# A hybrid RWKV-7, convolution and MoE layer on one core: reordered opening, moved masks, transposes and fills, and a third weight slot

## What is computed

```python
xn = rmsnorm(x, norm1_g)
z = xn @ w_in                      # 1024 x 7424: r | k | v | LoRA inputs | GLU (2 x 1024) | gates (2 x 1024)
zr_prev = previous token of z[:, :C_RWKV]           # samples: state_shift @ w_in
zm = zr + (zr_prev - zr) * mu_shift                 # r, k, v and three LoRA inputs
S = S * d_t + (S @ -kk_t) b_t^T + v_t k_t^T         # 16 heads, 64 x 64 state, per token
out_a = (groupnorm(S r_t) + bonus) * g
out_b = silu(layernorm(depthwise_conv(glu, width 31)))
h = x + (sigmoid(gA) * out_a + sigmoid(gB) * out_b) @ w_out
y = h + moe(rmsnorm(h, norm2_g))                    # top 8 of 64 experts and one shared expert
return rmsnorm(y), new states
```

## Time and profile before

| | us |
|---|---|
| median of 3 runs | 1151.5 |
| lowest, highest | 1150.77, 1154.52 |
| profiled execution | 1153.62 |
| its span, first to last instruction | 1151.8 |
| PE busy | 970.0 (84%) |
| DVE busy | 554.1 (48%) |
| POOL busy | 350.9 (30%) |
| ACT busy | 217.0 (19%) |
| mean granted TensorE clock | 0.929 of 2.4 GHz |

### The profile page before, as it was taken

The page is one execution under the profiler, slowest core; times in us unless marked ns, Lnnn a source line. Parts: engine busy times, 40 slices in busy tenths (PEclk is TensorE's granted clock), DMA queues, the critical chain, the costliest instruction groups (busy, mean ns, idle before and its releaser), DMA issues. The chain is left out here.

```text
span 1151.8 us, 17728 instructions
## 1 busy us (share of the span) xinstructions
PE 970.0 (84%) x7221; PEld 568.8 (49%) x7221; DVE 554.1 (48%) x1025; ACT 217.0 (19%) x460; POOL 350.9 (30%) x396
## 2 busy tenths in 40 slices
PE   4898899799889988579899888898888687969896
PEld 3677678767677776336633333333333233323231
DVE  2148758775884789675461111111111424333585
ACT  3231124112411421213011111111111111111002
POOL 0039705950892289000111101101112322222330
PEclk9998999899999999888999988988998888989899
DMA  8332354154306507383579999999999999999931
GB/s 249 122 110 84 126 163 129 48 185 151 111 19 220 159 3 264 126 342 152 207 278 401 417 417 413 415 414 400 408 403 399 412 409 368 406 406 402 389 101 39
DMA packets 98811, 295.65 MB, mean 257 GB/s; under 512 B 19570, under 2 KB 50740, under 8 KB 82071
## 3 DMA queue, kind: packets, MB, share of 16 engines
q1 hardware_dynamic: 80535, 254.02, 57.8%
q0 software_dynamic: 18192, 40.46, 9.7%
HBM read 284.12 MB, written 36.30 MB: 278 GB/s over the span
## 5 line engine op out<-in xcount | busy, mean ns | idle before, releaser
L1275 PE MATMUL bank<-big 64*64 64x64 f32 (+7 forms) x6778 | 914.6, 368 | 153.2 <-DMA big<-in_w_up 73.3
L1275 PEld LDWEIGHTS bank<-big 64*64 64x64 f32 (+3 forms) x6778 | 520.5, 154 | 497.9 <-issue 384.1
L1567 ACT ACTIVATE big<-bank 128x512 f32<-128x512 f32 (+11 forms) x292 | 124.7, 449 | 751.4 <-PE bank L1275 438.3
L1075 POOL DMA_INDIRECT big<-xg,big x32 | 32.4, 1013 | 405.2 <-PE bank L561 355.2
L2020 POOL TENSOR_SCALAR big<-big 128x256 f32<-128x256 f32 x120 | 129.0, 1075 | 0.4
L919 DVE TENSOR_TENSOR big<-big,bank 128x256 f32<-128x256 f32 x32 | 13.5, 421 | 234.6 <-ACT big L1567 234.6
L2032 POOL TENSOR_TENSOR big<-big 128x256 f32<-128x256 f32 x120 | 89.4, 745 | 0.3
L1845 DVE SCALAR_TENSOR_TENSOR big<-big 128x256 f32<-128x256 f32 x120 | 71.3, 594 | 4.0
L979 DVE SCALAR_TENSOR_TENSOR big<-big 128x1024 f32<-128x1024 f32 (+1 forms) x48 | 61.5, 1280 | 17.5 <-DMA big<-yrows,big 14.6
L1092 POOL DMA_INDIRECT big<-yrows,big x48 | 50.0, 1042 | 51.8 <-DVE big L979 29.5
L2016 POOL TENSOR_SCALAR big<-big 128x256 f32<-128x256 f32 x4 | 2.2, 551 | 190.5 <-DVE big L1805 190.5
(11 more groups left out here) (165 smaller groups left out, 439.5 us busy)
## 6 DMA issues: line engine op xcount, KB each, us to landing
big<-in_w_gate SPq DMA_DIRECT2D x64, 1024.0 KB, 16.1
big<-in_w_up SPq DMA_DIRECT2D x64, 1024.0 KB, 21.9
big<-in_w_down SPq DMA_DIRECT2D x64, 1024.0 KB, 15.3
big<-in_w_in SPq DMA_DIRECT2D x29, 1024.0 KB, 5.5
yrows<-big POOLq DMA_DIRECT2D x32, 512.0 KB, 6.2
big<-in_w_out SPq DMA_DIRECT2D x2, 2048.0 KB, 11.8
big<-in_x_prompt SPq DMA_DIRECT2D x2, 1024.0 KB, 7.0
big<-in_state_wkv SPq DMA_DIRECT2D x32, 64.0 KB, 2.3
```

The costliest lines, as they stand in the source:

```text
L1075: pool.indirect_dma_start(out=x[0:n, :], out_offset=None, in_=xg, in_offset=bass.IndirectOffsetOnAxis(ap=idxu[0:n, col:col + 1], axis=0), ...
L1275: return nc.tensor.matmul(out_, lhsT=lhsT, rhs=rhs, start=start, stop=stop)
L1567: return nc.scalar.activation(out_, in_, f, **kw)
```

## The change

It touches six things.

1. *Opening.* `rms_eps` moves up beside `ident`, and the first load takes only these 129 columns; the other 1421 are loaded with the LoRA weights, behind the second `w_in` piece, under the semaphore `late_in`. x is loaded in halves with the gains between. ACT makes one Sqrt before it waits for x. The waits for LoRA weights and `lora_ready` on PE move from before tile 2 to the first LoRA products. The copy of the convolution state leaves the opening (`shift_out` 48 becomes 32).
2. *Masks.* X2 moves from before the levels to behind the first Y.
3. *Transposes.* New `between`; `i % 8 % 3` starts each group with the same bank. ACT's copies follow the new order.
4. *State.* The memset of `S_st` moves ahead of T. PE's waits before the chunk loop are split up.
5. *Fills.* One after each odd tap 7 to 21; the state copy after tap 24 of group 3.
6. *Ring.* `NW` = 3.

```diff
-        NW = 2
+        NW = 3
@@ moe_pool: the fills and the state copy share one semaphore
-            pool.wait_ge(S['yrows_in'], 16 * NPAIR)
+            pool.wait_ge(S['yrows_in'], 16 * (NPAIR + 1))
@@ SP
-            sp.dma_start(const, A['const']).then_inc(S['consts_in'], 16)
-            sp.dma_start(xrow[:, 0:2, :], A['x_prompt'][0].rearrange("(t p) d -> p t d", p=128)) \
-              .then_inc(S['x_in'], 16)
+            sp.dma_start(const[:, 0:first], A['const'][:, 0:first]).then_inc(S['x_in'], 16)
+            sp.dma_start(xrow[:, 0, :], x_rows[:, 0, :]).then_inc(S['x_in'], 16)
+            sp.dma_start(grow, A['norm1_g'][0:1, :].partition_broadcast(128)).then_inc(S['small_in'], 16)
...
+            sp.dma_start(xrow[:, 1, :], x_rows[:, 1, :]).then_inc(S['hx_in'], 16)
...
-                sp.wait_ge(S['tr_free'], 8 * g + 2)
+                sp.wait_ge(S['tr_free'], 8 * g + 1)
...
                 if q == 1:
+                    sp.dma_start(const[:, first:], A['const'][:, first:]).then_inc(S['late_in'], 16)
@@ PE
             z_tile(0)
             z_tile(1)
-            pe.wait_ge(S['lora_in'], 48)
-            pe.wait_ge(S['lora_ready'], 3)
...
                 if g == 0:
                     pe.wait_ge(S['vec_ready'], 2)
+                    pe.wait_ge(S['late_in'], 64)
+                    pe.wait_ge(S['lora_ready'], 3)
...
-                pe.wait_ge(S['lmask_ready'], 4 * (g + 1))
+                pe.wait_ge(S['lmask_ready'], 4 * g + 2)
...
                 between = [
-                    lambda: (tr_units(BP), tr_samples(), tr_conv_state()),
+                    lambda: tr_samples(),
+                    lambda: (pe.wait_ge(S['lmask_ready'], 4 * (g + 1)), tr_units(BP)),
                     lambda: tr_units(KP),
                     lambda: tr_v(),
-                    lambda: tr_new_conv(),
-                    lambda: None,
+                    lambda: (tr_conv_state(), tr_new_conv()),
                 ]
...
-                pe.wait_ge(S['tt_ready'], 6 * g + 6)
-                pe.wait_ge(S['tr_free'], 8 * g + 6)
+                pe.wait_ge(S['tr_free'], 8 * g + 4)
                 pe.wait_ge(S['zero_ready'], g + 2)
...
                     pe.wait_ge(S['zq_ready'], n + 1)
+                    if c == 0:
+                        pe.wait_ge(S['tt_ready'], 6 * g + 6)
...
-                    if c:
-                        pe.wait_ge(S['o_ready'], n)
+                    pe.wait_ge(S['o_ready'], n) if c else pe.wait_ge(S['tr_free'], 8 * g + 6)
@@ ACT
-            act.wait_ge(S['consts_in'], 16)
-            act.wait_ge(S['x_in'], 16)
+            act.wait_ge(S['zero_ready'], 1)
+            fn(stat[:, 15:16], PP[:, 0, 0, 0:1], ACT.Sqrt)
+            act.wait_ge(S['x_in'], 32)
@@ DVE
-            dve.wait_ge(S['shift_out'], 48)
+            dve.wait_ge(S['shift_out'], 32)
...
+            dve.wait_ge(S['late_in'], 64)
             for g in range(NG):
...
+                note(v.memset(S_st[0], 0.0), 'zero_ready')
...
-                for h in range(2):
-                    dve.wait_ge(S['a_mm'], 5 * g + h + 4)
-                    note(v.tensor_tensor(X2[:, 4 * h:4 * h + 4],
...
                     link(v.tensor_tensor(Y_st, bank(0), bc(f'level{m}'), M), 'y_ready')
+                    if i == 0:
+                        for h in range(2):
+                            dve.wait_ge(S['a_mm'], 5 * g + h + 4)
+                            note(v.tensor_tensor(X2[:, 4 * h:4 * h + 4],
@@ POOL
-            pool.dma_start(out['conv_s'][0][:, 0:CW - 2, :], A['state_conv'][0][:, 1:CW - 1, :]) \
-                .then_inc(S['shift_out'], 16)
+            def fill(g, w):
+                i = (w - 7) // 2
+                if w % 2 and 0 <= i < NPAIR // NG:
+                    r = 2 * SLOTS * (NPAIR // NG * g + i)
+                    pool.dma_start(yrows[r:r + 2 * SLOTS, :], const[:, 0:D]).then_inc(S['yrows_in'], 16)
+                if g == NG - 1 and w == 24:
+                    pool.dma_start(out['conv_s'][0][:, 0:CW - 2, :], A['state_conv'][0][:, 1:CW - 1, :]) \
+                        .then_inc(S['yrows_in'], 16)
...
-                taps(g, 6, CW)
-                for i in range(NPAIR // NG):
-                    r = 2 * SLOTS * (NPAIR // NG * g + i)
-                    pool.dma_start(yrows[r:r + 2 * SLOTS, :], const[:, 0:D]).then_inc(S['yrows_in'], 16)
+                taps(g, 6, CW, lambda w: fill(g, w))
```

More of the change, by code:

```diff
@@ L76, in constants @@
     parts['ident'] = np.eye(128)
+    parts['rms_eps'] = np.full((128, 1), RMS_EPS)
     parts['same_head'] = (p[:, None] // 64 == p[None, :] // 64)
@@ L99, in constants @@
     parts['ln_eps'] = np.full((128, 1), LN_EPS)
-    parts['rms_eps'] = np.full((128, 1), RMS_EPS)
     off, cols = {}, 0
@@ L1282, in heads @@
                 return ins
-            pe.wait_ge(S['consts_in'], 16)
             for t in range(2):
@@ L1693, in _ @@
                 gate_tile(13)
+                copy_samples()
                 copy_units(BT_st)
-                copy_samples()
-                copy_conv_state()
                 copy_units(KTok_st)
                 copy_units(V_st)
+                copy_conv_state()
                 copy_new_conv()
@@ L1743, in _ @@
             v.memset(zs[:, :, 0:1], 0.0)
-            v.memset(C, 0.0)
             v.memset(UU[:, :, 0:CW - 1], 0.0)
             note(v.memset(PP[:, :, :, 0:1], 1.0), 'zero_ready')
+            v.memset(C, 0.0)
             dve.wait_ge(S['small_in'], 48)
@@ L1864, in _ @@
                 bank = lambda i: B[i][:, :].rearrange("p (u n) -> p u n", u=NU)
+                wait(dve, 's_mm', NCH * g)
+                wait(dve, 'o_mm', NCH * g)
+                wait(dve, 'tr_free', 8 * g)
+                note(v.memset(S_st[0], 0.0), 'zero_ready')
                 dve.wait_ge(S['a_mm'], 5 * g + 3)
@@ L1907, in sample_part @@
                         link(v.tensor_reduce(OS, SMT, AX.X, AD), 'os_ready')
-                wait(dve, 's_mm', NCH * g)
-                wait(dve, 'o_mm', NCH * g)
-                wait(dve, 'tr_free', 8 * g)
-                note(v.memset(S_st[0], 0.0), 'zero_ready')
-                dve.wait_ge(S['zero_ready'], g + 2)
                 for c in range(NCH):
@@ L2003, in _, with taps @@
             pool.dma_start(out['shift_s'][0], xrow[0:NS, 2, :]).then_inc(S['shift_out'], 16)
-            pool.dma_start(out['conv_s'][0][:, 0:CW - 2, :], A['state_conv'][0][:, 1:CW - 1, :]) \
-                .then_inc(S['shift_out'], 16)
-            def taps(g, w0, w1):
+            def fill(g, w):
[6 more added lines that the diff above has]
+                        .then_inc(S['yrows_in'], 16)
+            def taps(g, w0, w1, behind=None):
                 acc = C[:, 2 * g + 1, 0:NP]
@@ L2032, in taps @@
                     note(gp.tensor_tensor(acc, acc, TP[:, w % 3, :], ALU.add), 'tapm')
+                    if behind:
+                        behind(w)
+            pool.wait_ge(S['late_in'], 64)
             for g in range(NG):
```

29 lines of the change are left out of this document (15 added, 14 removed).

## The result

| | before | with the change |
|---|---|---|
| median of 4 executions, us | 1151.55 | 1139.38 |
| lowest, highest | 1150.77, 1154.52 | 1137.20, 1146.67 |
| profiled execution, its span | 1153.62, 1151.8 | 1146.67, 1144.9 |
| first products of groups 0, 1, 2, 3 | 76.03, 183.58, 291.13, 397.96 | 68.65, 172.84, 277.36, 382.97 |
| first expert weight issued | 493.11 | 477.24 |

The ratio is 0.988, 95% interval 0.986 to 0.991. Of the 27.4 forecast before the first expert weight, 15.9 came.

A forecast was written before the change was run, and what follows sets the result against it. PE's waits in the 493 us before the expert stage were taken as what to shorten; the DMA-busy expert stage would move forward as a block. 7.2 + 16.5 + 3.65 = 27.4 us gave 1124.1 us, range 1115 to 1136.

The forecast's parts named there:

- Part 1, the opening: Opening: earlier first weights 1.0, PE's 4.53 us gap gone, 1.7 from the clock; 7.2 us gained, bounded by 4 and 9.
- the third slot: Ring of w_in loads: the third slot itself earns nothing, since PE has no wait of note for w_in in the groups.
- Part 2, groups 0 to 2: Triangular inversion levels: moved masks, transposes and memset let PE start sooner; 4.4 us gained in each of these groups.
- The first gap: PE's wait before the first level: 2.0 us would be left.
- the t products: Levels, by group 1's clock: PE starts these products 4.8 us earlier.
- Part 2, group 3: Last group's levels: 3.3 us gained, without the 1.14 us before the chunk loop, as no projection tiles fill it.
- Part 3, the failing step: Fills between POOL's taps cost nothing, covered by idle time; PE's wait for od goes: 3.65 us, bounded by 0 and 5.
- DVE becomes the bound of the levels: Rival: DVE's work, slowed beside POOL, limits the levels; 2 us gained per group, 1132.6 us. Chance 0.17.
- Clock stays down: Rival: two scattered gaps hold PE's lower clock through the levels; 37 us slower, 1188 us. Chance 0.03.
- lost before the expert stage: Rival: another condition of the sync engine ends as late as now, so the gain vanishes; 1150 us. Chance 0.03.
- the clock stays up: Rival: PE keeps its upper clock in the levels, each group gaining 5.8 us; 1118.5 us. Chance 0.10.
- weight load behind the first was late in the opening: Rival: a weight load queues behind constants, LoRA weights and states; 5 us back, 1129 us. Chance 0.07.

The follow-up runs named there:

- opening_only: Kernel before with only the new opening, plus the convolution state copy moved behind tap 24 of group 3; 1145.3 us, ratio 0.994.
- fills_end: Changed kernel with only the fills of yrows put back to the end of each group; 1130.4 us, ratio 0.982.
- short_pool_taps: Changed kernel with POOL's taps cut to the first 8 tokens, fills still between them; 1114.7 us in one execution.
- wout_late: fills_end with w_out and the expert stage's x loaded only behind group 3's last y products; 1135.9 us, ratio 0.985.
- wout_after_od: fills_end with w_out, x and the router's loads issued behind the read-back of od of group 3; 1130.5 us, ratio 0.981.
- state_first: fills_end with DVE's sample step behind the state update and the copy of o, in group 3 only; 1131.5 us, ratio 0.981.
- wout_late_od_first: wout_late with group 3's fills issued only after od has been read back; 1126.4 us, ratio 0.977.
- again: The changed kernel run once more, unaltered; 1139.2 us, ratio 0.989.

## Why the prediction was wrong

- **Part 1, the opening: right.** 7.2 forecast; 7.4 in the profile, 7.1 by the medians of opening_only (the first products of group 0 lie between 67.6 and 69.2 us in all kernels with the new opening). The first tile came 1.6 us sooner (1.0 forecast). The gap between tiles 1 and 2 is gone, the granted clock is 1.00 from 20.2 to 60 us, the first tile came at 20.20, and the third slot earned nothing, as said.
- **Part 2, groups 0 to 2: right without the fills.** 4.4 a group forecast, 5.2, 5.1 and 4.3 in fills_end against opening_only. The first gap was 2.2 to 2.3 (forecast 2.0), the t products stood 4.5 earlier from the group's start (forecast 4.8), and no wait was left before the chunk loop. Whether the clock fell didn't matter for the first t: in group 3 the first y took 1.97 us or 1.34 (two kernels, same gap before), and the next gap was 0.73 or 1.35, so t began 3.24 and 3.25 us behind y. DVE's mask ends that wait, and a slow PE is hidden in it. By the rule of the Trainium skill ("TensorE: Matmul & The Clock Gate", section "HAM oscillation — how this bites in real kernels") the clock would have stayed up and each group gained 5.8. The trace doesn't agree: behind gaps of 2.15 to 2.29 us the clock fell in each group of fills_end, as in the kernel before, and the two best groups come near 5.8 through the order alone. What a clock that stays up gives is seen in short_pool_taps.
- **Part 2, group 3: wrong sign.** 3.3 forecast, 1.9 lost. I priced the moved steps on PE and DVE and left out what SP issues: its wait went from `8 * g + 2` to `8 * g + 1` and levels and transposes moved, so w_out was issued 31.3 us behind the group's start in fills_end instead of 36.1 before. PE then stood 1.97 + 0.77 us in the levels, and behind the first of these gaps the granted clock was 0.51 for 3 us. wout_late and wout_after_od removed exactly these gaps. That they are late fetches of PE's own instructions is an inference from the profile's "issue", not shown. The wait of 2.43 us for DVE before chunk 1 is a second cost; state_first moved it and gained nothing, so what it is worth stays open. The clock is a third: over the group it was 0.86 instead of 0.90, and the same products took PE 69.7 us instead of 66.9 in opening_only. With w_out and fills moved (wout_late_od_first) the group takes 90.1, 2.6 less than in opening_only; but 1.28 of this is the wait for `od`, so some 1.3 of the 3.3 came.
- **Part 3, the failing step.** "The taps end 4.3 us later, covered by the long idle time before POOL's first tap of the next group" costed the interleaved issues at nothing. They cost 8.8 us (again against fills_end): 3.2, 2.4 and 1.9 in groups 0 to 2 and 1.3 in group 3. I looked for who waits for the end of POOL's taps and not for who runs beside them. Group 1 shows the way: ten taps before the masks take 7.31 us instead of 6.24, so T is later, PE waits 3.5 instead of 2.3, and the rest is lost level by level. A part is the clock: over groups 0 and 1 of again and group 2 of the first profile it was 0.95 instead of 0.97, PE's products took 98.4 us instead of 97.0, and the same group is 0.3 to 1.3 us longer than in the other execution of the same kernel. And the 3.65 for `od` didn't need the move: fills_end has no wait for it, since its fills start 13.4 us before `od`, not 7.4 us as in the kernel before, and are over by then (the DMA engines are fully busy until 444 us, and at a share of 0.07 while `od` is written at 446).

By medians: 1152.35 (before), less 7.1 (opening), less 14.9 (levels, and what came free for `od`), plus 8.8 (fills between taps) is 1139.2. That is 13.2 of the 27.4 forecast: 8.8 of the 14.2 that are missing are the fills. The rest lies in group 3, where 3.3 + 3.65 was forecast and fills_end gained 0.6 against the kernel before; against this the groups 0 to 2 and the opening gave a little more than forecast. The profiles put 11.0, 12.2 and 8.5 before the first expert weight; why 4 us of the first don't show in the median of opening_only is open (its profile has 664.0 us behind the first weight, most others 657 to 661).

Of the rivals, "DVE becomes the bound of the levels" came nearest, with taps slowed beside POOL, and left 2 us a group as gain; the changed kernel gained 1.2 to 3.4 in groups 0 to 2 (2.0 to 2.7 in again). Its time of 1132.6 was still too low, as it counted 2 + 3.65 in group 3, where 0.9 came, and nothing in again. "Clock stays down" did not occur (0.95 to 0.97 over groups 0 to 2), and neither did "lost before the expert stage" or "the clock stays up"; no weight load behind the first was late in the opening.

## To carry to other kernels

When transfers move between the compute instructions of GpSimd, ask what VectorE does in those microseconds, even if GpSimd has 40 us to spare: here eight issues of 0.61 us a group made VectorE's taps a fifth longer, on the path that bounds the stage. Put bulk transfers where they are over before a small, awaited transfer (`od`), or behind it; a lead of 7.4 us was too short for 4 MB, 13.4 us was enough. And price a part by its own run before the parts are put together: two good ones and a bad one looked like one fair change.

## What the runs showed of the hardware

- A GpSimd transfer issue between two-input instructions lengthens VectorE's instructions that follow (taps 600 to 725 ns), with 64 bytes a row (716 ns) as with 4 KB, while a memset of 0.52 to 0.93 us doesn't (609 to 615 ns).
- Without POOL's long taps DVE's take 493 ns, and groups 0 to 2 are 2.5 to 3.3 us shorter than in fills_end. So much the two engines' collisions still cost there, in part through the clock: PE's products alone are 1.7 to 2.3 us shorter at a granted clock of 1.00.
- Behind a gap of PE of 2.15 to 2.29 us the granted clock fell in every group of fills_end (0.56 over the next 5 us in group 1); behind 0.54 to 0.60 us it stayed at 1.00 in groups 0 to 2 of short_pool_taps.
- PE can stand 0.5 to 2.3 us with nothing to wait for while a bulk load runs (1.97 and 0.77 in fills_end); the gaps go when the load moves.
- 8 KB for `od` took 1.4 us with the DMA engines at a share of 0.07, 4.6 and 6.9 with fills issued from 9.8 and 7.4 us before it, 7.9 behind fills and w_out (wout_late).
